# Two transformer blocks on one core: three more weight panels' first halves at each norm border, and the sums of squares one panel behind

## The reference, cut to what matters

```python
h = rms_norm(x, g_pre) ...; z = h @ w_in         # then mixing branches
y = concat(branches) @ w_out
x = x + gt * rms_norm(y, g_post)                 # a border of the kernel
h = rms_norm(x, g_pre_ffn) * (1 + sc) + sh       # the next product needs the norm of the new x
up = dwconv3(h @ w_up); gate, val = split(up)    # block 1: width 3 convolution, gelu(gate) * val
y = (gelu(gate) * val) @ w_down
x = x + gt_f * rms_norm(y, g_post_ffn)           # border, then block 2: its own w_in_2, branches,
                                                 # w_out_2, border, relu(h @ w_up)**2 @ w_down_2, end
```

## Time and profile before

| what | value |
|---|---|
| median of 3 runs | 3016.02 us (3013.66 to 3024.22) |
| the profiled execution's own time | 3020.56 us |
| its span | 3018.8 us |
| mean granted clock of TensorE | 0.962 |
| TensorE busy | 2816.0 us, 93% |
| DVE, ACT, POOL busy | 41%, 28%, 29% |
| DMA | 240.22 MB, mean 80 GB/s |

### The profile page before, as it was taken

One profiled execution on the slowest core, in us unless ns is written; L12 is line 12 of the kernel. 1 busy time (PEld: TensorE's weight loads), 2 busy tenths in 40 slices (PEclk: granted clock), 3 DMA queues, 4 the chain that ended last, 5 costly groups with the idle time before them and its releaser, 6 DMA issues.

```text
span 3018.8 us, 31426 instructions
## 1 busy us (share of the span) xinstructions
PE 2816.0 (93%) x13134; PEld 2184.7 (72%) x13134; DVE 1228.2 (41%) x1572; ACT 854.6 (28%) x1288; POOL 867.0 (29%) x412
## 2 busy tenths in 40 slices
PE   6888889799999999978999999999879999999996
PEld 3656647588888888757777777777667888888875
DVE  6646612565435353455656422221443112111115
ACT  4413643332212121234453221111343112222112
POOL 1322113334334242342111121111244333333333
PEclk8999999899999999988999999999989999999998
DMA  5453254211111111312113121111312111111113
GB/s 225 178 132 97 64 209 165 105 42 56 42 49 45 47 54 45 108 67 98 43 49 105 56 79 53 53 52 52 125 63 98 49 49 56 49 49 40 45 49 140
DMA packets 84845, 240.22 MB, mean 80 GB/s; under 512 B 10592, under 2 KB 25440, under 8 KB 84704
## 3 DMA queue, kind: packets, MB, share of 16 engines
q1 hardware_dynamic: 76672, 213.48, 20.5%
q10 hardware_dynamic: 4608, 14.92, 1.3%
q0 software_dynamic: 3424, 9.81, 0.9%
HBM read 201.63 MB, written 36.54 MB: 79 GB/s over the span
## 4 chain that ended last, share of the span: by engine, by line
PE 83%; DVE 7%; ACT 3%; issue 3%; DMA 2%; POOL 2%; SPq 1%; ACTq 0%; POOLq 0%; DVEq 0%
PE ps L1265 24%; PE ps L1266 23%; PE ps L1267 23%; PE pc L1621 3%; PE pss L1571 1%; POOL whl L2794 1%; PE pss L1234 1%; PE ps L1482 1%; DVE y L1639 1%; PE ps L1428 1%; PE ps L1303 1%; DMA adaw<-in_w_ada 1%; DVE y L1645 1%; ACT act L2358 1%; POOL y L2794 1%
## 5 line engine op out<-in xcount | busy, mean ns | idle before, releaser
L2794 POOL TENSOR_TENSOR whl<-wraw,whl 128x1024 fp32r<-128x1024 f32 (+1 forms) x238 | 617.2, 2596 | 1647.7 <-ACT whl L2358 1647.5
L1265 PE MATMUL ps<-act,whl 128*128 128x512 f32 x2464 | 1000.8, 406 | 42.4 <-DVE act L1645 10.0
L1266 PE MATMUL ps<-act,whl 128*128 128x512 f32 x2464 | 973.3, 395 | 0.0
L1267 PE MATMUL ps<-act,whl 128*128 128x512 f32 x2464 | 972.9, 395 | 0.0
L1265 PEld LDWEIGHTS ps<-act,whl 128*128 128x128 f32 x2464 | 469.4, 191 | 185.7 <-issue 72.0
L1266 PEld LDWEIGHTS ps<-act,whl 128*128 128x128 f32 x2464 | 469.8, 191 | 105.8 <-issue 8.9
L1267 PEld LDWEIGHTS ps<-act,whl 128*128 128x128 f32 x2464 | 468.7, 190 | 103.8
L1265 PE MATMUL ps<-hid,whl 128*128 128x512 f32 x864 | 343.9, 398 | 20.4 <-issue 11.6
L1266 PE MATMUL ps<-hid,whl 128*128 128x512 f32 x864 | 341.8, 396 | 0.0
L1267 PE MATMUL ps<-hid,whl 128*128 128x512 f32 x864 | 339.1, 393 | 0.0
L2358 ACT ACTIVATE whl<-wraw 128x1024 fp32r<-128x1024 f32 (+1 forms) x238 | 246.7, 1037 | 300.7 <-PE ps L1267 274.0
(11 more groups left out here) (302 smaller groups left out, 2481.0 us busy)
## 6 DMA issues: line engine op xcount, KB each, us to landing
wraw<-in_w_in SPq DMA_DIRECT2D x60, 512.0 KB, 3.5
wraw<-in_f1u SPq DMA_DIRECT2D x44, 512.0 KB, 3.5
wraw<-in_f2d SPq DMA_DIRECT2D x36, 512.0 KB, 3.4
wraw<-in_w_out SPq DMA_DIRECT2D x32, 512.0 KB, 3.5
x<-in_w_ada SPq DMA_DIRECT2D x32, 512.0 KB, 6.6
wraw<-in_f2u SPq DMA_DIRECT2D x32, 512.0 KB, 3.4
xs<-y SPq DMA_DIRECT2D x24, 512.0 KB, 3.4
x<-in_xT ACTq DMA_DIRECT2D x16, 512.0 KB, 8.8
```

The costliest lines, as they stand in the source:

```text
L1265: pe.matmul(PSB[g.bank][:, :], hi, src[:, 0, k, c], start=e == 0, stop=False)
L1266: pe.matmul(PSB[g.bank][:, :], hi, src[:, 1, k, c], start=False, stop=False)
L1267: m = pe.matmul(PSB[g.bank][:, :], lo, src[:, 0, k, c], start=False, stop=e == len(ks) - 1)
L2794: return g_.tensor_tensor(out, a, b, op)
```

## The change

- `EARLY` names three more panels for each of the three borders: 3, 4, 5 of f1u and of f2u, and 9, 7, 11 of w_in2. `heads` makes their half-0 tiles first, each from a panel that is let go at once, and then the old three. The stage later streams these three panels again and makes only their half 1. The early results of f1u and f2u go to spare buffers (`early`, `late`); when the panel's turn comes ACT copies them into `pad` or `rl` (one more ACT instruction each). Those of w_in2 go to their final place.
- `use_sq` has a ring of three buffers (two for s = 5), and `add_sums` takes a condition. In `residual` of half 0, `r_sum` of group j is put behind `r_add` and `r_sq` of group j + 1.
- The yields: 1.4 after each `r_add` becomes 2.2 in half 0 and 1.8 in half 1, and half 0 has 1.0 more ahead of `r_rows2`.
- At the end (s = 5), half 0: POOL adds x for all 8 groups, not only for the odd ones.
- The apply's temporary buffers of s = 1 and 4 are three instead of four.

```diff
+EARLY = {"f1u": (3, 4, 5), "w_in2": (9, 7, 11), "f2u": (3, 4, 5)}
...
-    [("w_in", i) for i in W_IN_ORDER] + [("w_out", i) for i in range(8)] * 2 + ffn_order("f1", 22, 2)
-    + [("w_in2", i) for i in range(52)]
-    + [("w_out2", i) for i in range(8)] * 2 + ffn_order("f2", 32, 1)
+    [("w_in", i) for i in W_IN_ORDER] + [("w_out", i) for i in range(8)] * 2 + [("f1u", i) for i in EARLY["f1u"]] + ffn_order("f1", 22, 2)
+    + [("w_in2", i) for i in range(55)]
+    + [("w_out2", i) for i in range(8)] * 2 + [("f2u", i) for i in EARLY["f2u"]] + ffn_order("f2", 32, 1)
...
-            self.put("ev", self.tile(kind, i, n, 0))
+            if (kind, i) not in self.early:
+                self.put("ev", self.tile(kind, i, n, 0))
...
     def heads(self, kind, idxs, out):
+        for i in EARLY[kind]:
+            n = self.panel(kind, i)
+            t = self.tile(kind, i, n, 0)
+            self.put("ev", t)
+            self.panel_done(n, t)
+            self.early.add((kind, i))
...
-        ring = self.sq.setdefault(s, [0, [None, None]])
-        b = ring[0] % 2
+        size = 2 if s == 5 else 3
+        ring = self.sq.setdefault(s, [0, [None] * size])
+        b = ring[0] % size
         ring[0] += 1
+        self.add_sums(lambda entry: entry[3] == b)
...
-            yield 1.4
-            p.add_sums()
+            if j:
+                p.add_sums(lambda entry: entry[2] < j)
+            yield 1.8 if half else 2.2
...
         yield 1.0
+        p.add_sums()
         if half:
             p.put("r_sum", s, half, *sums.pop(0))
+        else:
+            yield 1.0
...
+        def add_on_pool(s, half, j):
+            return j % 2 == 1 or (s == 5 and half == 0)
...
+                elif (g.kind, g.i) in plan.early and g.kind != "w_in2" and half == 0:
+                    m = av(early[g.kind][g.i - 3], b[:, :], ACT.Copy if g.kind == "f1u" else ACT.Relu)
...
+                    if (g.kind, g.i) in plan.early:
+                        av(pad[g.i % 3][:, 1:513], early[g.kind][g.i - 3], ACT.Copy).then_inc(*mark("erA", "f1", g.i))
```

More of the change, by code:

```diff
@@ L216, in __init__ @@
         self.sums = []
+        self.early = set()
         self.now = 0.0
@@ L364, in use_sq, with add_sums @@
         return b, free
-    def add_sums(self):
-        while self.sums:
+    def add_sums(self, due=lambda entry: True):
+        while any(map(due, self.sums)):
             self.put("r_sum", *self.sums.pop(0))
     def norm_add(self, s, half, j, t):
-        self.add_sums()
         b, free = self.use_sq(s, ("nd", s, half, j))
@@ L1060, in projection_bufs @@
             ss[s] = sb(f"ss{s}", [P, T], c=c)
-            sqb[s] = [sb(f"sq{s}{b}", [P, 512], c=c)[:, :] for b in range(2)]
-            tmp[s] = [sb(f"tm{s}{b}", [P, 512], c=c)[:, :] for b in range(4)]
-            sb(f"over{s}", [P, 3096], c=c)
+            sqb[s] = [sb(f"sq{s}{b}", [P, 512], c=c)[:, :] for b in range(3)]
+            tmp[s] = [sb(f"tm{s}{b}", [P, 512], c=c)[:, :] for b in range(1)]
+            sb(f"over{s}", [P, 1024 + 3096], c=c)
+            tmp[s] += [sb(f"tn{s}{b}", [P, 512], c=c)[:, :] for b in range(2)]
             diag[s] = sb(f"diag{s}", [P, 512], c=c)[:, :]
@@ L1080, in build @@
         diag[2] = sb("diag2", [P, 512], c=c4)[:, :]
+        late = sb("late", [P, 512], c=c4)[:, :]
         c4.close()
+        c5 = ExitStack()
+        sb("before", [P, 76 * 256], c=c5)
+        early = sb("early", [P, 2, 512], c=c5)
+        c5.close()
+        early = {"f1u": [early[:, 0, :], early[:, 1, :], late]}
         X[2] = X[5] = XA
@@ L1084, in build @@
         ss[2] = pad[2]
-        sqb[2] = [cv[:, 512 * h:512 * h + 512] for h in range(2)]
+        sqb[2] = [cv[:, 512 * h:512 * h + 512] for h in range(2)] + [late]
         pb2 = ExitStack()
@@ L1120, in build @@
         rl = [sb(f"rl{b}", [P, T], c=c9) for b in range(3)]
+        sb("over5", [P, 24], c=c9)
         ss[5] = sb("ss5", [P, T], c=c9)
@@ L1124, in build @@
         diag[5] = rl[0][:, 0:512]
+        early["f2u"] = early["f1u"][0:2] + [sqb[5][1]]
         def col(name, i=0, n=1):
@@ L1167, in split_done @@
             return done("msP" if j % 4 == 3 else "msD", half, j)
+        def add_on_pool(s, half, j):
+            return j % 2 == 1 or (s == 5 and half == 0)
         def added_done(s, half, j):
-            return done("raP" if j % 2 else "raD", s, half, j)
+            return done("raP" if add_on_pool(s, half, j) else "raD", s, half, j)
         def x_done(s, j):
@@ L1207, in build, with up_done @@
         up_tile = {"f1": panel_tiles("f1u"), "f2": panel_tiles("f2u")}
+        def up_done(name, i):
+            out = [done("evA", up_tile[name][i, h]) for h in range(2)]
+            return out + ([done("erA", name, i)] if (name + "u", i) in plan.early else [])
         down_tile = {}
@@ L2000, in r_add @@
                     *mark("raD", "t", s, half, j))
-                if j % 2 == 0:
+                if not add_on_pool(s, half, j):
                     w.wait_ge(*x_done(s, j))
@@ L2056, in h1_gate @@
                 w.wait_ge(*done("h1D", "pad", 2))
-                for h in range(2):
-                    w.wait_ge(*done("evA", up_tile["f1"][2 * i, h]))
+                for d in up_done("f1", 2 * i):
+                    w.wait_ge(*d)
                 if i:
@@ L2064, in h1_val @@
                 a, b = 2 * i % 3, (2 * i + 1) % 3
-                for h in range(2):
-                    w.wait_ge(*done("evA", up_tile["f1"][2 * i + 1, h]))
+                for d in up_done("f1", 2 * i + 1):
+                    w.wait_ge(*d)
                 x = pad[a][:, 1:T + 1]
@@ L2075, in h2 @@
                 x = rl[i % 3][:, :]
-                for h in range(2):
-                    w.wait_ge(*done("evA", up_tile["f2"][i, h]))
+                for d in up_done("f2", i):
+                    w.wait_ge(*d)
                 tt(x, x, x, ALU.mult).then_inc(*mark("h2D", i))
@@ L2473, in ev @@
                         w.wait_ge(*done("hidP", "f2", g.i - 3))
+                    if (g.kind, g.i) in plan.early:
+                        av(rl[g.i % 3][:, 0:512], early[g.kind][g.i - 3], ACT.Copy).then_inc(*mark("erA", "f2", g.i))
                     m = av(rl[g.i % 3][:, c], b[:, :], ACT.Relu)
@@ L2855, in r_add @@
             def r_add(s, half, j):
-                if j % 2:
+                if add_on_pool(s, half, j):
                     c = HALF[half]
```

## The result

| | before | changed |
|---|---|---|
| median | 3019.26 us (4 runs, 3013.66 to 3024.22) | 3000.62 us (4 runs, 2997.04 to 3002.84) |
| ratio | | 0.9932, 95% interval 0.9916 to 0.9948 |
| profiled execution, span | 3018.8 us | 2997.2 us |

A forecast was written before the change was run, and what follows sets the result against it. TensorE, busy 93% of the span, was taken as the bound. Gains of 0.3 us at s=1, 20.3 at s=2, 8.7 at s=4 and 2 at the end made 31: 3016 - 31 = 2985 us, range 2956 to 3008.

The forecast's parts named there:

- Part 1, s = 1 and 4: New yields and later sums, up to half 1's broadcast: 3 us gained at s=1, 5 at s=4.
- Part 1, s = 2: New yields and later sums at s=2, up to half 1's broadcast: 14 us gained.
- 11 to remain of these 25: At s=2, 18.4 us idle plus about 7 lost to the clock would fall to 11, gaining 14.
- Part 2: Three early tiles beside half 1's chain: next stage's half 1 starts 11.7 us later at each border.
- Part 3, s = 1: Behind the s=1 border: 3.3 us of clock back and 5.7 of the 16.4 us moved work usable.
- PE waits of some 10 us in total: Sign expected at the start of f1, within 60 us, the waits ended by ACT or POOL.
- Part 3, s = 2: Behind the s=2 border: 3.0 us of clock back and 15.0 from work already done.
- Part 3, s = 4: Behind the s=4 border: 2.0 us of clock back and 13.4 from work done, 3 taken off for POOL.
- Part 4: At the end, POOL adds x for all groups of half 0: 2 us gained, range -3 to 3.2.
- the waits go altogether: Rival: a loop shorter than 7.3 us leaves no waits at the row sums; 62 us gained, 2954; chance 0.20.
- the later sums shorten nothing: Rival: ACT's order and POOL's port set the loop, no border gains up to half 1's broadcast; 9 us, 3007; chance 0.15.
- slower: Rival: stages bound by work from their first half-1 evacuation, early tiles only delay it; -25 us, 3041; chance 0.07.

The follow-up runs named there:

- e2: The kernel before with only the three early panels a border added; yields, sums, ring and end as before: 3013.17 us, ratio 0.9961.
- e12: The kernel before with only the last yield of half 0 at s=1 and 4 raised from 1.0 to 14.6: 3016.03 us, ratio 0.9967.
- e1: The changed kernel without any early panels, keeping its yields, later sums, ring and end: 3013.39 us, ratio 0.9965.
- e3: The changed kernel without early panels at s=1 (f1u), those of s=2 and 4 kept: ratio 0.9903, 30.0 us faster than before.
- e6: The changed kernel with one early panel a border instead of three and half 1's groups one k-step apart: 2994.99 us, ratio 0.9901.

## Why the prediction was right and where it was wrong

The sign of every part was right, and the mechanism of most. By its own steps, with the two profiles of the changed kernel:

- **Part 1, s = 1 and 4: right, sizes a little under.** Forecast +3 and +5; measured +2.1 and +2.9 in the first profile, +3.2 and +3.6 in the second. The wait of 15.3 fell to 7.4 (forecast 6.4), the turn to 7.4 us (7.3), the new waits are 5.9 and 3.7 (5 and 2). The wait is 7.4 and not 6.4 because the last sum came some 1 us earlier than before, not 2. Each new wait brought a stretch at 1.2 GHz, as forecast. The sums do not close: 8.9 off the long wait, less 5 or 2 for the new one and 3 for its clock, are 0.9 and 3.9, and the prediction names nothing for the rest of its +3 and +5. The trace does: the waits of 2.0 between the tiles (s = 1) and of 1.5 ahead of `r_bc` (both) are gone.
- **Part 1, s = 2: the term that failed.** Forecast +14; measured +6.8 against the profile of before and 3.8 against two others with its code. The step was "11 to remain of these 25". What remained was 21.5: PE idle 15.8 us, not some 4, and 11.4 us of its work at 1.2 GHz, half of which, 5.7, is what the clock cost. The 25 were themselves 28.5, since in the kernel before PE did 20.2 us of its work there at 1.2 GHz, a loss of 10.1 and not 7; in e2 and e12 it was 5 beside 20 of idle time. I counted 1.3 for the diagonal and 2.3 for the activations and took DVE to be ready when PE arrives. The trace has four waits of 1.3 to 2.5 between the tiles of half 1 (at 1305, 1312, 1321 and 1326 us), 1.7 at `r_rows2` and 4.5 at the diagonal. Most of the 4.5 is this row, an instruction that takes 0.69 us alone, beside POOL:

```profile
1340.42 2.63 DVE L1671 TENSOR_TENSOR diag<-ident,rcol 128x512 f32<-128x512 f32 x1
...
1345.21 1.40 DVE L1677 SCALAR_TENSOR_TENSOR pad<-y,par,pss 128x512 f32<-128x512 f32 x2 [2.17 <-PE pss L1548]
```

- **Part 2: right.** Forecast 11.7 later at each border; measured 11.1, 10.9 and 9.6. POOL's and ACT's work and the loads hid: PE was idle 0.4 us at most.
- **Part 3, s = 1: the number right, in part by luck.** Forecast 3.3 + 5.7 = 9.0; measured 8.1 and 6.6. "PE waits of some 10 us in total": 8.7 and 8.5, so 7.7 of the 16.4 were usable and not 5.7. Against that the clock gave back little of its 3.3: before, 6.1 us ran at 1.2 GHz behind R; now 3.4 do in the first profile and 6.8 in the second, behind the new waits. The way that the loop reaches PE was another too. The forecast took the size from the bank of panel 8; the four waits stand at the starts of the four panels right behind the interleaved tiles, and each ends 0.1 us behind POOL's low part of a panel. ACT makes the high parts late, behind steps of f1 for which it waited 3.6, 5.8 and 6.2 us for DVE. The trace names them "issue"; the third of them:

```profile
647.53 2.79 POOL L2832 TENSOR_TENSOR whl<-wraw,whl 128x1024 fp32r<-128x1024 f32 x1
650.42 0.77 PE L1297 MATMUL ps<-act,whl 128*128 128x512 f32 x1 [2.97 <-issue]
```

- **Part 3, s = 2: under-sized.** Forecast 18.0; measured 22.0 and 20.5. Some 200 us behind the border, in the recurrent branches, every kernel without an early w_in2 panel has two waits, 5.3 us together (before, e1, e12), and at least 3.4 us at 1.2 GHz; every kernel with one has a wait of 1.2 to 1.5 there and full clock. I had looked only at the border itself. How one early panel does this was not followed further.
- **Part 3, s = 4: right.** 2.0 + 13.4 = 15.4 forecast, 14.2 measured; the 3 us taken off for POOL were 2.5 to 2.7 of idle PE.
- **Part 4: right.** +2 forecast; PE's idle time at the end fell from 11.9 to 9.8 in all kernels that have it, and the wait of 6.2 to 4.0. The loss of up to 3 us that was worked out there from the rule of the Trainium skill (SBUF — State Buffer, "Who interferes with whom") did not come. The rule itself shows: beside POOL's additions of 1.3 us two of DVE's sums took 1.2 us for 0.69 (at 2963.35 and 2972.48), but that is 1 us together, and POOL's last low part of a weight panel (2.40) had ended at 2959.8, ahead of its first addition.

So the terms sum to 27.5 in the first profile, or 24.5 with the 3 us of clock at s = 2 taken out, against 31. Part 1 fell 10 us short of its 22, and parts 2 to 4 came out 6.4 better than forecast, which hides more than half of that. The medians gave 18.6, with an interval of 15.7 to 25.4 us, and 24.7 on the other chip: 24.5 agrees with both. The rivals: "the waits go altogether" fails on the waits of 7.4; "the later sums shorten nothing" fails on the loop; "slower" is out. Two of the prediction's numbers around them do not follow from its text: "slower" leaves out the 22 us of part 1, with which it is -3 and not -25; and the range starts at 2956, next to the first rival's 2954, while half way into it is 2970.

What the prediction did not see, though its numbers said it, is that the three tiles are three edits. It had 4.7 us to fill and 5.46 of work in a tile, so one tile was enough, and the usable 5.7 at f1 is again one tile. Two thirds of part 2 and part 3 only move work across R.

## What to carry to other kernels

Work that is brought forward into a stall is worth the stall it fills and the clock behind it, not its own length: count tile by tile and stop where the stall is full. Before an engine's wait is attacked by shortening the chain, look at what stands behind the late step in every other queue: here the place of one step in the order was worth 17.5 us, as it gave PE ten k-steps more ahead of the sums and ACT the last tiles ahead of apply. In the kernel before, where PE then ran out of weight panels, it was worth 8. And lay two traces over each other at the same matmul. In this case the stretches of like code agreed to 1 or 2 us and their idle time mostly to 0.3, where medians of five rounds tell some 4; where the clock fell differently, as at s = 2 and ahead of s = 4, they were 2.5 to 3 us apart.

## What the runs showed of the hardware

- DVE beside POOL: a sum of 0.69 us took 2.68, the diagonal 2.63, an addition 2.48, each ending some 0.5 us behind POOL's instruction of 2.4. DVE's multiply, with an input in PSUM, took 0.73 to 0.75 in all 32 places of the changed kernel, 21 of them beside POOL. That is the rule of the Trainium skill (SBUF — State Buffer, "Who interferes with whom") for instructions with two inputs in SBUF. A plain copy, which has one, was held too:

```profile
519.04 0.74 DVE L1677 SCALAR_TENSOR_TENSOR y<-y,gmod,pc 128x512 f32<-128x512 f32 x1
519.70 2.40 DVE L2045 COPY ss<-sq 128x512 f32<-128x512 f32 x1
522.02 0.73 DVE L1677 SCALAR_TENSOR_TENSOR y<-y,gmod,pc 128x512 f32<-128x512 f32 x1
```

  The same copy took 0.43 us without POOL. By the same section of the Trainium skill copies can enter a mode that takes both ports; this row agrees.
- Six row sums of eight small matmuls one behind the other cost 1.04 us each; with nine matmuls between them 0.89 (2.94 us from one to the next at s = 1, less 9 x 0.2275).
- The same wait is not always followed by the same clock: 3.4 us of idle PE ahead of s = 4 had no stretch at 1.2 GHz behind it in the profiles of before, e1 and e3, and 6.8 us of it in the first of the changed kernel, in e6 and in e12, which has the code of before there; that stretch was 2.5 us longer.
